# Decoder step on one core: K, V and U weight tiles in other slots, K and V cache pages issued one by one, vectors before x, three x chunks turned first

## What is computed

```python
h = rmsnorm(x, norm1_g)
z = h @ w_in                                   # 2048 x 4096
q, k, v, u = split(z, [1024, 2048, 3072])
a = attend(q, k, v)      # prompt: causal; samples: 3 best of 8 cached blocks of 256 keys, and their own
p, new_hist = pool_mixer(u, hist, start_pos, w_pool, pool_scale)
x = x + concat([a, p]) @ w_out
h2 = rmsnorm(x, norm2_g)
x = x + (silu(h2 @ w_gate) * (h2 @ w_up)) @ w_down   # inner width 5632
y = rmsnorm(x, norm_f_g)
```

## Time and profile before

| what | us |
|---|---|
| median of 3 runs (1454.62 to 1457.8) | 1457.61 |
| the profiled execution, its own time | 1456.8 |
| its span, first to last instruction | 1455.0 |
| PE busy in the span | 1396.7 (96%) |
| DVE busy | 902.3 (62%) |
| ACT busy | 501.1 (34%) |

### The profile page before, as it was taken

How to read it: one execution, slowest core, us unless ns; L and a number is a source line. 1 busy time by engine, 2 the same in 40 slices (tenths; PEclk the granted TensorE clock), 3 DMA queues, 4 the chain that set the end, 5 groups by cost and what they waited for, 6 DMA issues and landing times.

```text
span 1455.0 us, 34098 instructions
## 1 busy us (share of the span) xinstructions
PE 1396.7 (96%) x13900; PEld 1294.7 (89%) x13900; DVE 902.3 (62%) x1355; ACT 501.1 (34%) x663; POOL 105.7 (7%) x180
## 2 busy tenths in 40 slices
PE   6999999998898999999999999999999999999998
PEld 5987777767555789999999999999999999999997
DVE  4777777767777645787555464646464646455556
ACT  4421221121134234644343433333333333333334
POOL 2127600000000000200000000000000000000002
PEclk9998999999999999999999999999999999999999
DMA  5898999999999865655655555555555555555552
GB/s 189 264 323 294 361 400 403 401 397 393 395 389 369 275 196 179 199 163 176 189 161 170 161 171 161 170 161 169 162 168 164 167 165 165 167 164 168 164 168 95
DMA packets 164616, 334.41 MB, mean 230 GB/s; under 512 B 10271, under 2 KB 54488, under 8 KB 164223
## 3 DMA queue, kind: packets, MB, share of 16 engines
q1 hardware_dynamic: 164519, 333.06, 68.0%
HBM read 328.10 MB, written 5.27 MB: 229 GB/s over the span
## 4 chain that ended last, share of the span: by engine, by line
PE 81%; SPq 9%; DVE 4%; issue 3%; DMA 3%; ACT 1%; DVEq 0%; ACTq 0%
PE banks L1469 24%; PE banks L1470 24%; PE banks L1471 24%; SPq L427 3%; PE banks L1584 3%; SPq L431 3%; PE banks L1566 2%; SPq L449 2%; DMA vpage<-in_cache_v 2%; PE banks L1477 1%; DVE kpage L897 1%; SPq L419 1%; PE banks L1650 1%; DMA vec<-in_pool_scale 1%; PE banks L1600 1%
## 5 line engine op out<-in xcount | busy, mean ns | idle before, releaser
L855 DVE TENSOR_TENSOR w_lo<-w_raw,w_hi 128x1024 fp32r<-128x1024 f32 x360 | 440.9, 1231 | 405.1 <-ACT w_hi L587 404.2
L1469 PE MATMUL banks<-hh,w_hi 128*128 128x288 f32 x2176 | 646.6, 297 | 4.0 <-issue 1.5
L1470 PE MATMUL banks<-hl,w_hi 128*128 128x288 f32 x2176 | 645.1, 296 | 0.0
L1471 PE MATMUL banks<-hh,w_lo 128*128 128x288 f32 x2176 | 642.8, 295 | 0.6 <-issue 0.6
L587 ACT ACTIVATE w_hi<-w_raw 128x1024 fp32r<-128x1024 f32 x360 | 378.7, 1058 | 671.5 <-PE banks L1471 449.6
L1469 PEld LDWEIGHTS banks<-hh,w_hi 128*128 128x128 f32 x2176 | 411.3, 189 | 21.8 <-issue 18.1
L1470 PEld LDWEIGHTS banks<-hl,w_hi 128*128 128x128 f32 x2176 | 411.4, 189 | 1.1 <-issue 1.0
L1471 PEld LDWEIGHTS banks<-hh,w_lo 128*128 128x128 f32 x2176 | 410.3, 189 | 0.6 <-issue 0.6
L1471 PE MATMUL banks<-ah,w_lo 128*128 128x288 f32 x704 | 207.8, 295 | 0.0
L1470 PE MATMUL banks<-al,w_hi 128*128 128x288 f32 x704 | 207.4, 295 | 0.0
L1469 PE MATMUL banks<-ah,w_hi 128*128 128x288 f32 x704 | 206.6, 293 | 0.5 <-DVE al L1288 0.5
(11 more groups left out here) (197 smaller groups left out, 642.5 us busy)
## 6 DMA issues: line engine op xcount, KB each, us to landing
kpage<-in_cache_k SPq DMA_DIRECT2D x128, 512.0 KB, 7.9
vpage<-in_cache_v SPq DMA_DIRECT2D x128, 512.0 KB, 7.1
w_raw<-in_w_gate SPq DMA_DIRECT2D x88, 512.0 KB, 3.6
w_raw<-in_w_up SPq DMA_DIRECT2D x88, 512.0 KB, 3.6
w_raw<-in_w_down SPq DMA_DIRECT2D x88, 512.0 KB, 3.7
w_raw<-in_w_in SPq DMA_DIRECT2D x64, 512.0 KB, 9.3
w_raw<-in_w_out SPq DMA_DIRECT2D x32, 512.0 KB, 4.1
xs<-in_x_prompt SPq DMA_DIRECT2D x2, 1024.0 KB, 7.2
```

The costliest lines, as they stand in the source:

```text
L855: V.tensor_tensor(w_lo[:, s, :], w_raw[:, s, :], w_hi[:, u, :].bitcast(F32), ALU.subtract).then_inc(lo_ready, 1)
L1469: PE.matmul(o, wh, xh[:, c, :], start=start and i == 0, stop=False)
L1470: PE.matmul(o, wh, xl[:, c, :], start=False, stop=False)
L1471: last = PE.matmul(o, wl, xh[:, c, :], start=False, stop=stop and i == len(chunks) - 1)
```

## The change

**Start.** Only the first 128 columns of `tab` are loaded first, then the vectors, then x; the other 1154 columns follow after q tile 1 of the loads, and PE waits for them ahead of q tile 8. `X_AHEAD` is 3.

**Pages.** K pages of slots 0 and 1 go out with q tiles 4 to 11, V quad 0 with q tiles 12 to 15, one page each, and V quad 1 with KVU tiles 0 to 3.

**KVU tiles.** `KVU_COUNT` says how many each of the 24 slots has, after tiles 0 and 1: slots 0, 1 and 2 have one instead of two, slot 3 three, slots 5 and 6 one, slots 14, 15 and 18 three, slot 23 one instead of none, all others two as before. So by the end of slot 2 three tiles fewer are done than before, after slot 3 two, and from slot 6 to slot 13 four. Where a slot holds a block's end ahead of its last tile, its tiles are parted there (`split_at_block`): DVE takes the block and splits the rest ahead of turning the next K, and PE puts `values` between. In slot 23 the tile comes ahead of `values`, and all four `rows_turned` come after them.

```diff
-X_AHEAD = 6
+X_AHEAD = 3
...
+KVU_COUNT = (1, 1, 1, 3, 2, 1, 1, 2, 2, 2, 2, 2, 2, 2, 3, 3, 2, 2, 3, 2, 2, 2, 2, 1)
+KVU_FIRST = 2
+KVU_AT = [range(KVU_FIRST + sum(KVU_COUNT[:n]), KVU_FIRST + sum(KVU_COUNT[:n + 1])) for n in range(len(KVU_COUNT))]
+BLOCKS_IN = [[k // 4 for k in tiles if k % 4 == 3] for tiles in KVU_AT]
...
+def split_at_block(n):
+
+    first = BLOCKS_IN[n][0] if BLOCKS_IN[n] and KVU_AT[n][-1] % 4 != 3 else -1
+    return [k for k in KVU_AT[n] if k // 4 == first], [k for k in KVU_AT[n] if k // 4 != first]
...
-            sp.dma_start(tab[:, :], A["tables"][:, 0:at["rel"][0]]).then_inc(tab_in, 16)
+            sp.dma_start(tab[:, 0:P], A["tables"][:, 0:P]).then_inc(tab_in, 16)
+            for n, name in enumerate(("norm1_g", "norm2_g", "norm_f_g", "pool_scale")):
+                g = A[name] if name == "norm_f_g" else A[name][0]
+                sp.dma_start(vec[16 * n:min(16 * n + 16, 56), :], g.rearrange("(c p) -> c p", p=P)).then_inc(vec_in, 16)
...
             for k in range(16):
                 c, j = k // 8, k % 8
+                if k == 2:
+                    sp.dma_start(tab[:, P:at["rel"][0]], A["tables"][:, P:at["rel"][0]]).then_inc(tab_in, 16)
...
-                if k == 6:
+                if k == 4:
                     sp.wait_ge(pages_in, 16)
-                if 6 <= k < 14:
-                    load_k_page((k - 6) // 4, (k - 6) % 4)
-            for k in range(4):
+                if 4 <= k < 12:
+                    load_k_page((k - 4) // 4, (k - 4) % 4)
+                if k == 12:
+
+                    sp.wait_ge(xT_in, KC)
+                    sp.wait_ge(hist_T, 2)
+                if k >= 12:
+                    load_v_page(0, k - 12)
+            for k in range(KVU_AT[1][-1] + 1):
                 load_kvu(k)
-            load_v(0)
-            load_v(1)
-            load_kvu(4)
-            load_kvu(5)
+                if k < 4:
+                    load_v_page(1, k)
...
-                for k in (2 * n + 6, 2 * n + 7):
-                    if k < KVU_TILES:
+                if n + 2 < len(KVU_AT):
+                    for k in KVU_AT[n + 2]:
                         load_kvu(k)
...
             for i in range(KVU_STEPS):
-                lo_kvu(4 * i + 1)
+                n = NQUADS * i
+                lo_kvu(KVU_AT[n])
...
-                take_block(2 * i)
-                lo_kvu(4 * i + 2)
-                turn_k(i, 2)
-                lo_kvu(4 * i + 3)
-                turn_k(i, 3)
-                take_block(2 * i + 1)
-                lo_kvu(4 * i + 4)
...
+                slot_ends(n)
+                for j in (1, 2):
+                    head, tail = split_at_block(n + j)
+                    lo_kvu(head or tail)
+                    if head:
+                        slot_ends(n + j)
+                        lo_kvu(tail)
+                        turn_k(i, j + 1)
+                    else:
+                        turn_k(i, j + 1)
+                        slot_ends(n + j)
+                head, tail = split_at_block(n + 3)
+                lo_kvu(head or tail)
                 scaled_logits(i)
                 pad_q(i + 1)
...
-                kvu_tile(8 * i + 2)
+                tiles = KVU_AT[NQUADS * i]
+                kvu_tile(tiles[0])
                 if i:
                     joint_max(i - 1)
-                kvu_tile(8 * i + 3)
+                for k in tiles[1:]:
+                    kvu_tile(k)
...
                     logits(i, j)
-                    if i == KVU_STEPS - 1 and j == NQUADS - 1:
-                        pe.wait_ge(z_ready, 24)
-                        rows_turned(0)
-                        rows_turned(1)
+                    head, tail = split_at_block(NQUADS * i + j)
+                    last_slot = i == KVU_STEPS - 1 and j == NQUADS - 1
+                    for k in tail if last_slot else head:
+                        kvu_tile(k)
                     if i:
                         values(i - 1, j - 1)
-                    kvu_pair(4 * i + j + 1)
+                    for k in () if last_slot else tail:
+                        kvu_tile(k)
                 if i == KVU_STEPS - 1:
+                    pe.wait_ge(z_ready, 24)
+                    rows_turned(0)
+                    rows_turned(1)
                     rows_turned(2)
                     rows_turned(3)
```

More of the change, by code:

```diff
@@ L626, in _, with hi_kvu @@
                 hi(tile_at(4 + k))
-            def hi_kvu(pair):
-                if 2 * pair < KVU_TILES:
-                    for k in (2 * pair, 2 * pair + 1):
-                        hi(tile_at(T_KVU + k))
+            def hi_kvu(tiles):
+                for k in tiles:
+                    hi(tile_at(T_KVU + k))
             def save_comb(b):
@@ L696, in mixed @@
                 copy(hh[:, c, :], nrm[:, r % 2, :]).then_inc(y_hi, 1)
-            hi_kvu(0)
+            hi_kvu(range(KVU_FIRST))
             for i in range(KVU_STEPS):
-                hi_kvu(4 * i + 1)
+                hi_kvu(KVU_AT[NQUADS * i])
                 if i >= 2:
@@ L886, in x_taken, with lo_kvu @@
                 V.tensor_copy(xT[:, c, :], XB[c % 3][:, 0:T]).then_inc(x_ready, 1)
-            def lo_kvu(pair):
-                if 2 * pair < KVU_TILES:
-                    for k in (2 * pair, 2 * pair + 1):
-                        lo(tile_at(T_KVU + k))
+            def lo_kvu(tiles):
+                for k in tiles:
+                    lo(tile_at(T_KVU + k))
             def turn_k(i, j, pages_=range(4)):
@@ L923, in _ @@
                     turn_k(0, 0)
-                    lo_kvu(0)
+                    lo_kvu(range(KVU_FIRST))
                 if k % 8 == 7:
@@ L1086, in _, with slot_ends @@
             pad_q(0)
+            def slot_ends(n):
+                for m in BLOCKS_IN[n]:
+                    take_block(m)
             for i in range(KVU_STEPS):
-                lo_kvu(4 * i + 1)
+                n = NQUADS * i
+                lo_kvu(KVU_AT[n])
                 if i:
@@ L1518, in _ @@
                     pe.wait_ge(ext_ready, 2)
+                    pe.wait_ge(tab_in, 32)
                     sum_sq(0)
@@ L1661, in own_logits @@
                 last.then_inc(so_in, 1)
-            def kvu_pair(pair):
-                if 2 * pair < KVU_TILES:
-                    kvu_tile(2 * pair)
-                    kvu_tile(2 * pair + 1)
-            kvu_pair(0)
+            for k in range(KVU_FIRST):
+                kvu_tile(k)
             replicate_q()
```

38 lines of the change are left out of this document (22 added, 16 removed).

## The result

The changed kernel took 1459.07 us (median of 12 runs, 1455.31 to 1461.34), the kernel before 1456.42 beside it: a ratio of 1.0017, 95% interval 1.0010 to 1.0025. Repeated on another chip it was 1459.59 against 1457.28, 1.0016 (1.0007 to 1.0026). It is slower by about 2.4 us, where 6.8 us faster was forecast (1450.4, range 1447 to 1453.5).

What follows compares the result with a forecast made beforehand. PE was taken to bound the q tiles and bytes at 400 GB/s the stage from 160 us; 13.0 us of lead less 5.2 for bytes left 7.8, and 7.8 - 2.0 + 1.0 = 6.8 us faster gave 1450.4 us, range 1447 to 1453.5.

Steps and rivals of the forecast that it cites:

- What bounds the kernel: PE bounds the q tiles; from 160 to 385.4 us bytes do, at 400 GB/s.
- B: Steps 3 to 5: PE becomes the bound, using only some two thirds of its free time; 1455 us, chance 13%.
- D: Steps 3 to 5: PE's free 17.8 us cannot be filled, so it pays all four tiles; 1461 us, chance 5%.
- A: Stage goes by slot turnaround, not bytes, and the whole 13.0 us lead stays; 1443.8, say 1444 us, chance 10%.
- Start, +1.5: Up to the first logits: first q tile 3.1 us earlier, 1.6 back for chunks; lead 1.5 us (0 to 3).
- Step 0 and slot 4: Up to logits 5: 6.5 us from fewer tiles, 1.8 of wait, 3.9 of clock, less 0.7; lead 13.0 (8 to 14).
- lost at half clock: 130.2 to 144.6 us: 9.8 us stood at half clock; 3.9 us taken as gained if the wait stays short.
- Bytes, -5.2: After logits 5: four tiles' 2.10 MB still to come, 5.2 us at 400 GB/s, leaving 7.8 us of lead.
- Three-tile slots, -2.0: Slots 14 to 18: SP waits for tile buffers, so transfers idle for 2 us (bounds 0 and 4).
- End of step 5, +1.0: After logits 23: PE's 4.52 us wait shrinks and values may avoid half clock; 1.0 us gained (-3 to +2).
- Rival C: Thinned slots: waits for K drop PE to half clock; lead about 0 after bytes and the rest, 1457 us, chance 8%.
- what will show it: Signs: first q tile at 17 to 18.5 us, logits 5 at 131 to 132, 400 GB/s until about 379, logits 24 about 383.

Runs made afterwards that it cites:

- v_late_cut: Kernel before, one V page in each of slots 12 to 15 loaded for 16 of 128 rows, 1.84 MB fewer: 1454.42 against 1456.81 us, 0.9983.
- pe_late_cut: Kernel before, 8 of 24 matmuls left out in KVU tiles 26, 28, 30 and 32, all bytes kept: ratio 1.0007 (0.9998 to 1.0016).
- start_only: Kernel before with only the new order of table, vectors and x, and `X_AHEAD = 3`: ratio 0.9999 (0.9990 to 1.0008).
- the six traces: Six profiles with the changed kernel's tile table, two of them the changed kernel itself; three have the new start, three the new page order: logits 5 at 140.8 us.
- k_cut_after: Changed kernel, K pages of slots 2 to 4 loaded for 16 of 128 rows: logits 5 at 135.75 us against 142.60; no whole time given.
- start_tiles: Changed kernel with the page order of the kernel before: 1458.90 us, ratio 1.0016 (1.0007 to 1.0025) to the kernel before.
- last_slot_free: Changed kernel with slot 23's tile moved to slot 20: ratio 1.0011 (1.0003 to 1.0020) to the kernel before, 1.0 us under the changed kernel.
- before_again: Kernel before, unedited, profiled a second time: own time 1458.42 us.
- repay_early: Changed kernel with its third tiles in slots 10, 11, 13 and 14: 1459.91 us, ratio 1.0024 (1.0015 to 1.0033) to the kernel before.
- shift_in_step0: Changed kernel with two tiles per slot except one in slot 2, three in slot 3, none in slot 23: ratio 1.0011 (1.0002 to 1.0020).

## Why the prediction was wrong, point by point

**What bounds the kernel: right.** Bytes, from 160 us on (v_late_cut against pe_late_cut). The Trainium skill, DMA: Bandwidth & Descriptors, "Where 436 GB/s comes from", puts the ceiling of the 16 ports at 435; no window of 36 us or more here is above 404. Rivals B and D have PE short of time in the changed kernel. By their own sign (transfers under 390 GB/s from 230 to 380) they fall: over 196 to 385 the changed kernel moves 398 and PE has 12.4 us without work; pe_late_cut says so for the kernel before only. Yet D's 1461 is the nearest time given. A falls: no lead of 13 us ever stood.

**Start, +1.5: mis-sized, 0.1.** Over all 20 traces the first q tile begins at 20.9 us with the old start (9 traces) and 18.3 with the new (11), 2.6 us earlier where 3.1 was forecast. It runs at half clock at its begin in both and takes 4.6 to 5.9 us in both, so the second q tile still has 2.5 us (27.2 and 24.7). Logits 0 stand at 90.7 and 90.6. The lead is lost in between: 5.5 pairs of chunks now lie between tiles, against 4, which costs 1.9 us from the second tile to logits 0 in start_only (65.2 us against 63.3 in the first trace of the kernel before) where 1.6 was taken, and nine of the 11 traces with the new page order have a wait of 0.2 to 1.2 us for a tile's split at 80 to 82 us that none with the old order has.

**Step 0 and slot 4, the step that failed.** The prediction's 13.0 at logits 5, less the start's 1.5, was 43.4 us from logits 0 to 5; the six traces have 50.1. By slots:

| stretch | forecast | measured | what it missed |
|---|---|---|---|
| slots 0 to 2 | 3 x 6.0 + 0.7 = 18.7 | 22.4 | K's turnaround, DVE's order in slot 2, half clock in slot 0 (two traces of six) |
| slot 3 | 13.8 | 14.5 | the wait left at logits 4 |
| slot 4 | 14.4 - 3.9 = 10.5 | 13.2 | DVE's block choice under the half clock |

In a thin slot PE's work no longer covers the round from a logits' end to the quad two further: from 95.95 (logits 0 done, at half clock) to 107.10 are 11.2 us of asking, landing and turning, with one slot of work in between. The forecast compared the slot only with its bytes, 6.6 us. The 3.9 us "lost at half clock" was for the most part not on the path: without any half clock slot 4 takes 12.7 us (k_cut_after, start_tiles, last_slot_free), and the profiled 14.4 of the earlier trace rows was itself long. before_again has 13.0; its PE in slot 4:

```profile
131.75 4.07 PE L1584 MATMUL banks<-kpage,qr 32*32 32x256 f32 x128 [3.06 <-DVE kpage L897]
...
139.98 0.38 PE L1545 MATMUL banks<-dm,tab 128*128 128x4 f32 x2 [0.55 <-DVE dm L988]
```

Here the clock was back sooner and PE waited for `dm`; in the first trace `dm` was ready when the slow tile ended. Missing are 1.4 from the start and 3.7 + 0.7 + 2.7 = 7.1 from the slots, 8.5 in all, which takes 13.0 to 4.5; measured 4.6. (The three forecasts sum to 43.0; the 0.4 up to 43.4 is left over in the prediction's rounded terms.)

**Bytes, -5.2: borne out, as far as the marks can tell.** 4.5 us of lead with four tiles owed (logits 12), 0.8 with one owed (3 x 1.3 = 3.9 paid: 0.6 expected), -1.0 when all are paid (-0.7 expected). From logits 8 on the other marks scatter about this by up to 3 us (7.3 at logits 11, -0.5 to -0.2 at logits 19 to 22 with one owed).

**Three-tile slots, -2.0: about half of it.** Logits 14 to 16 take 32.0 us in all six traces against 26.6 on average in the even ones, 5.4 for two tiles whose bytes are 2.6, and the lead falls to -0.5; by logits 23 it is back where bytes put it. But the transfers fall short by 1.0 us from 240 to 280, as shown, inside the forecast's bounds of 0 and 4. The marks can't resolve 1 us, so they don't gainsay it. Placed in four slots close together (repay_early) the window loses 2.1 us.

**End of step 5, +1.0: not gained; a loss, if any, is small.** Tile 47 waited for its split in all six traces and in three of them ran at half clock as well, 1.5 us more. From logits 23 to 24 it is 16.3 us on average with moved tiles and 14.5 with even ones; of these 1.8 us 1.3 are the tile's bytes, so about 0.5 us were lost, within the bounds of -3 and +2. last_slot_free has 1.0 us, not clear of noise.

**Rival C** (half clock in thinned slots) was partly true: 0.91 in 80 to 100, 0.76 in 130.2 to 144.6. Its time of 1457 doesn't follow from its own terms, though: -2.9 + 5 - 5.2 for the bytes and -1.0 for the rest is -4.1, hence 1461. In the changed kernel logits 0 and 4 took 4.03 and 3.84 us instead of 2.76, behind waits of 1.79 and 1.87 us; yet the same 1.79 us left logits 0 at 2.75 in the earlier trace rows and in 17 of the 20 traces. The earlier wait at 80 to 82 us doesn't part them: shift_in_step0 has 1.20 us of it and logits 0 at full clock. The Trainium skill, TensorE: Matmul & The Clock Gate, "HAM oscillation — how this bites in real kernels", describes such falls behind waits for DMA; the traces agree in part: here PE waited for DVE, some waits of this length are followed by half clock and others not, and the fall in slot 4 costs little because another engine ends last. Of "what will show it", the first q tile (18.49; 18.0 to 18.6 in all traces with the new start), SP's waits (to 6.1 us) and the 398 GB/s came; logits 4, 5 and 24 did not.

No version tried that computes everything beats the kernel before. A split that is shared with another engine at the end of step 0 was not tried.
